# Inverse row sums of the attentions over 64 partitions by two DMAs through DRAM, not by products on PE

## What is computed

```
first block, each of 2 layers:
    q, k, v and gates of four branches from x @ w_in
    A: banded chunk attention with a relative bias, 4 heads    M: attention over 256 memory rows, 4 heads
    C: banded chunk attention with sinks, 4 heads              B: latent attention, chunk-causal, 4 heads
    y = concat(branch * silu(gate)) @ w_out;  x = layer_norm(alpha * x + y)
second block, each of 2 layers:
    Fourier mix of 512 channels, windowed attention with sinks over the other 512 (8 heads)
    x = x + concat(rms(y_f), rms(y_a)) @ w_o;  x = x + (silu(conv(gate)) * conv(val)) @ w_down
softmax of a head:  p = exp(s - max) / sum(exp(s - max));   out = p @ v
```

## Time and profile before

| | |
|---|---|
| median of the runs | 1791.63 us |
| time of the profiled execution | 1798.1 us |
| its span, first to last instruction | 1796.0 us |
| mean granted clock of TensorE | 0.963 of full |
| PE, DVE, ACT, POOL busy | 1721.2, 780.9, 695.8, 677.4 us |
| DMA | 145.90 MB, mean 81 GB/s |
| chain that ended last | PE 67%, issue 20%, POOL 7%, others 6% |

### The profile page before, as it was taken

The page is one execution under the profiler, slowest core; times in us unless marked ns, Lnnn a source line. Parts: engine busy times, 40 slices in busy tenths (PEclk is TensorE's granted clock), DMA queues, the critical chain, the costliest instruction groups (busy, mean ns, idle before and its releaser), DMA issues.

```text
span 1796.0 us, 24207 instructions
## 1 busy us (share of the span) xinstructions
PE 1721.2 (96%) x8858; PEld 1349.8 (75%) x8858; DVE 780.9 (43%) x1496; ACT 695.8 (39%) x1144; POOL 677.4 (38%) x523
## 2 busy tenths in 40 slices
PE   6999999999999979999999999999998999999999
PEld 5776567787656757877888888888776888888887
DVE  7225554501555363664455215432556355403541
ACT  4443462524446141554344223333345344313431
POOL 3431314443131352334444444434252544444443
PEclk9998998999999878998999999999998999999999
DMA  7220112222011112122232232223120322233222
GB/s 257 99 72 24 51 46 97 92 98 92 25 49 47 65 42 71 48 72 71 84 103 82 88 111 93 76 88 118 48 72 27 103 98 99 72 97 115 93 72 92
DMA packets 24608, 145.90 MB, mean 81 GB/s; under 512 B 3152, under 2 KB 3536, under 8 KB 10704
## 3 DMA queue, kind: packets, MB, share of 16 engines
q1 hardware_dynamic: 21840, 138.01, 22.4%
q10 hardware_dynamic: 2688, 6.82, 1.0%
HBM read 142.72 MB, written 2.10 MB: 81 GB/s over the span
## 4 chain that ended last, share of the span: by engine, by line
PE 67%; issue 20%; POOL 7%; ACT 2%; DVE 2%; DMA 1%; POOLq 0%; ACTq 0%; DVEq 0%
PE ring L513 58%; POOL w_lo L499 7%; PE scores L561 2%; PE ring L585 2%; PE outs L575 2%; PE ring L655 1%; PE ring L599 1%; DMA xt<-in_x 1%; PE ring L629 1%; PE ring L917 1%; ACT probs L1066 0%; ACT w_hi L1021 0%; ACT xh L1248 0%; ACT xt L1244 0%; DVE g L1561 0%
## 5 line engine op out<-in xcount | busy, mean ns | idle before, releaser
L499 POOL TENSOR_TENSOR w_lo<-w_stage,w_hi 128x258 fp32r<-128x258 f32 (+5 forms) x471 | 643.8, 1397 | 1075.5 <-ACT w_hi L1021 674.6
L513 PE MATMUL ring<-xh,w_lo 128*128 128x512 f32 x1296 | 521.3, 402 | 23.4 <-DVE w_lo L1439 10.7
L513 PE MATMUL ring<-xh,w_hi 128*128 128x512 f32 x1296 | 514.6, 397 | 0.0
L513 PE MATMUL ring<-xl,w_hi 128*128 128x512 f32 x1296 | 513.9, 397 | 0.0
L513 PEld LDWEIGHTS ring<-xh,w_lo 128*128 128x128 f32 x1296 | 246.4, 190 | 86.4 <-DVE w_lo L1439 10.7
L513 PEld LDWEIGHTS ring<-xh,w_hi 128*128 128x128 f32 x1296 | 246.2, 190 | 56.2
L513 PEld LDWEIGHTS ring<-xl,w_hi 128*128 128x128 f32 x1296 | 246.9, 191 | 53.5
L1370 ACT ACTIVATE w_hi<-w_stage 128x2048 fp32r<-128x2048 f32 (+2 forms) x70 | 116.6, 1666 | 158.8 <-PE ring L513 158.8
L1380 ACT ACTIVATE g<-ring,convw 128x512 f32<-128x512 f32 x88 | 68.1, 778 | 245.4 <-DVE ring L1871 245.4
L1021 ACT ACTIVATE w_hi<-w_stage 128x2064 fp32r<-128x2064 f32 (+2 forms) x81 | 123.5, 1537 | 95.0 <-PE ring L513 94.4
L1066 ACT ACTIVATE probs<-scores,neg_max 128x256 f32<-128x256 f32 (+2 forms) x192 | 96.1, 503 | 147.7 <-DVE neg_max L1533 36.4
(11 more groups left out here) (268 smaller groups left out, 2245.1 us busy)
## 6 DMA issues: line engine op xcount, KB each, us to landing
w_stage<-in_mixed SPq DMA_DIRECT2D x62, 1032.0 KB, 4.8
w_stage<-in_up SPq DMA_DIRECT2D x44, 1024.0 KB, 4.8
w_stage<-in_down SPq DMA_DIRECT2D x16, 768.0 KB, 4.2
w_stage<-in_down SPq DMA_DIRECT2D x16, 640.0 KB, 3.8
xt<-in_x ACTq DMA_DIRECT2D x4, 512.0 KB, 11.4
out_t<-xt ACTq DMA_DIRECT2D x8, 256.0 KB, 2.0
mem_f<-in_mem SPq DMA_DIRECT2D x1, 1024.0 KB, 9.6
bias_r<-in_relb SPq DMA_DIRECT2D x1, 1024.0 KB, 11.3
```

Of the source, the lines that this page charges most:

```text
L499: ins = nc.gpsimd.tensor_tensor(w_lo[:, slot, cols], source[:, cols], w_hi[:, slot, cols].bitcast(F32), ALU.subtract)
L513: ins = nc.tensor.matmul(o, lhs, rhs, start=start, stop=stop, skip_group_check=True)
```

## The change

Of each attention all output tiles but the last (o % 8 != 7 in the first block, o % 4 != 3 in the second; 20 of 24) get their rows in another way:

- ACT, one step after the last exponentials of the tile and behind the exponentials of that step, waits for the reciprocal and issues a DMA of the 128 x 8 inverse sums to a DRAM scratch of (2, 8, 128), transposed, so 1024 pieces of 4 bytes (`send_sums`).
- ACT, one step later and again behind the exponentials, waits until that DMA has landed and issues two DMAs that read 512 numbers of one head from the scratch onto 64 partitions each (`fetch_rows`). The rows go to `vb` or `raw`, which are free then, or in the second block straight to `g`.
- PE's `spread_heads` and its ring bank are gone for these tiles, in the second block ACT's copy of the bank too.
- DVE in the first block multiplies the output bank in place by the rows and then by the gate, two products one behind the other, in place of the product of gate and bank and the product of output and gate. All of it, and the work that follows it on ACT and DVE, is one step later than before; for tile 6 of a layer of the first block the split by ACT and DVE moves from the shared list of units to this place.

```diff
+def rows_by_dma(o):
+    return o % 8 != 7 if o < 8 * DEPTH else o % 4 != 3
@@ ring_plan and PE's attention
-            if t >= 2 and (t - 2) % TT == TT - 1:
+            if t >= 2 and (t - 2) % TT == TT - 1 and not rows_by_dma(pairs[t - 2][0]["o"]):
@@ build
+        sums_rows = nc.dram_tensor("sums_rows", (2, 8, P), F32).ap()
+        dma_tiles = [o for o in range(12 * DEPTH) if rows_by_dma(o)]
+        def row_buffer(o):
+            if o >= 8 * DEPTH:
+                return g[:, 4 + o % 4, :]
+            if o % 8 < 2:
+                return vb[:, 2 * (o % 2):2 * (o % 2) + 2, :].rearrange("p a b -> p (a b)")
+            return raw[:, 2 * (o % 2), :]
@@ ACT
+            def send_sums(o):
+                if rows_by_dma(o):
+                    act.wait_ge(S("inv_ready"), o + 1)
+                    act.dma_start(sums_rows[o % 2].rearrange("c q -> q c"), row_inv[:, o % 2, :],
+                                  allow_slow_non_contiguous=True).then_inc(S("sums_sent"), 16)
+            def fetch_rows(o, l):
+                if rows_by_dma(o):
+                    act.wait_ge(S("sums_sent"), 16 * (dma_tiles.index(o) + 1))
+                    if o < 8 * DEPTH and o % 8 == 2:
+                        act.wait_ge(S("lat_split"), 3 * l + 3)
+                    for par in range(2):
+                        act.dma_start(row_buffer(o)[64 * par:64 * par + 64, :], bass.AP(sums_rows.tensor, (o % 2 * 2 + par) * TOK, [[0, HD], [1, TOK]])
+                                      ).then_inc(S("rows_landed"), 16)
...
-                    if t >= 2 and (t - 2) % TT == TT - 1:
-                        take_sums(pairs[t - 2][0])
-                    if t >= 4 and (t - 4) % TT == TT - 1:
-                        after_out(pairs[t - 4][0])
+                    if 1 <= t <= N and pairs[t - 1][0]["qt"] == TT - 1:
+                        send_sums(pairs[t - 1][0]["o"])
+                    if 2 <= t <= N + 1 and pairs[t - 2][0]["qt"] == TT - 1:
+                        fetch_rows(pairs[t - 2][0]["o"], l)
+                        if not rows_by_dma(pairs[t - 2][0]["o"]):
+                            take_sums(pairs[t - 2][0])
+                    for late in (4, 5):
+                        if late <= t < N + late and (t - late) % TT == TT - 1 and rows_by_dma(pairs[t - late][0]["o"]) == (late == 5):
+                            after_out(pairs[t - late][0])
...
+                    act.wait_ge(S("out_taken"), 8 * l + 2)
                     for n in range(2):
                         for t in (2 * n, 2 * n + 1):
                             evac(("uv", l, t), vb[:, t, :], cols=slice(0, 256))
...
-                    for n in range(7):
+                    for n in range(6):
                         split_out(l, n)
@@ DVE
-                    if scale_gate and t >= 2 and (t - 2) % TT == TT - 1:
+                    if scale_gate and t >= 2 and (t - 2) % TT == TT - 1 and not rows_by_dma(pairs[t - 2][1]["o"]):
                         scale_gate(pairs[t - 2][1])
-                    if t >= 3 and (t - 3) % TT == TT - 1:
-                        finish(pairs[t - 3][1], 0)
-                    if t >= 4 and (t - 4) % TT == TT - 1:
-                        finish(pairs[t - 4][1], 1)
+                    for part in range(2):
+                        for late in (3 + part, 4 + part):
+                            if late <= t < N + late and (t - late) % TT == TT - 1 and rows_by_dma(pairs[t - late][1]["o"]) == (late == 4 + part):
+                                finish(pairs[t - late][1], part)
...
+            def rows_ready(it):
+                if rows_by_dma(it["o"]):
+                    dve.wait_ge(S("rows_landed"), 32 * (dma_tiles.index(it["o"]) + 1))
+                else:
+                    wait_taken(dve, ("bc", it["o"]))
+                dve.wait_ge(S("pv_done"), it["n"] + 1)
...
                     if part == 0:
-                        wait_taken(dve, ("bc", it["o"]))
-                        dve.wait_ge(S("pv_done"), it["n"] + 1)
+                        rows_ready(it)
+                        if rows_by_dma(it["o"]):
+                            gates_taken(n)
+                            o = o_bank[it["o"] % 2]
+                            step(v.tensor_tensor(o[:, :], o[:, :], row_buffer(it["o"]), ALU.mult))
                         v.tensor_tensor(g[:, tile, :], o_bank[it["o"] % 2][:, :], g[:, tile, :], ALU.mult).then_inc(S("out_taken"), 1)
```

More of the change, by code:

```diff
@@ L565, in attention @@
                         it = pair[0]
-                        if (t - 2) % TT == TT - 1:
+                        if (t - 2) % TT == TT - 1 and not rows_by_dma(it["o"]):
                             spread_heads(it["o"])
@@ L1052, in rotary_tables @@
                 act.wait_ge(S("sines"), 4)
+            def send_sums(o):
[11 more added lines that the diff above has]
+                                      ).then_inc(S("rows_landed"), 16)
             def attention(pairs, l, block, take_sums, after_out, between):
                 N = len(pairs)
-                for t in range(N + 4):
+                for t in range(N + 5):
                     if t >= 1:
@@ L1212, in later_projections @@
                             yield
-                attention(PAIRS[l], l, 1, lambda it: None, lambda it: split_out(l, 7) if it["o"] % 8 == 7 else None, later_projections())
+                attention(PAIRS[l], l, 1, lambda it: None, lambda it: split_out(l, it["o"] % 8) if it["o"] % 8 >= 6 else None, later_projections())
                 ahead = l + 1 < DEPTH
@@ L1638, in later_projections, with gates_taken @@
                             yield
-                def scale_gate(it):
-                    n, tile, name = it["o"] % 8, it["tile"], ("bc", it["o"])
+                def gates_taken(n):
                     if n in (0, 2):
@@ L1649, in scale_gate @@
                         wait_taken(dve, ("w", l, f"bg{n - 6}"))
+                def scale_gate(it):
+                    tile, name = it["tile"], ("bc", it["o"])
+                    gates_taken(it["o"] % 8)
                     wait_full(dve, name)
@@ L1655, in gate_pair @@
                     if part == 0:
-                        wait_taken(dve, ("bc", it["o"]))
-                        dve.wait_ge(S("pv_done"), it["n"] + 1)
+                        rows_ready(it)
[3 more added lines that the diff above has]
+                            step(v.tensor_tensor(o[:, :], o[:, :], row_buffer(it["o"]), ALU.mult))
                         v.tensor_tensor(g[:, tile, :], o_bank[it["o"] % 2][:, :], g[:, tile, :], ALU.mult).then_inc(S("out_taken"), 1)
-                    elif n == 7:
+                    elif n >= 6:
                         out_lo(l, n)
```

## The result

| | median of the runs | lowest to highest | runs |
|---|---|---|---|
| before | 1792.17 us | 1790.54 to 1794.35 | 4 |
| after | 1882.95 us | 1878.12 to 1887.09 | 4 |

After stands to before as 1.0509, with an interval of 1.0496 to 1.0522: 5.1% slower, where 0.7% faster was forecast. The profiled execution of the changed kernel has a span of 1882.2 us, against 1796.0 before.

The account below looks back on a forecast made before the run. Attentions were taken as bound mostly by PE's stream, in a few steps by ACT or DVE. Gross gain 24.4 us less 9.8, 1.2 and 0.4 gave 13 us: 1791.6 - 13 = 1778.6 us, range 1766 to 1792.

Parts of the forecast that it names:

- Part 5: Landing of the sums' 1024 pieces of 4 bytes in DRAM, which ACT awaits: 4 us taken, costing 0.4 us in all.
- high end: Upper estimate of the sums' landing: 64 pieces on each of 16 engines 6.8 us, with 2.0 us fixed 8.8 us.
- The rival: Landing late, ACT stands in the fetch and PE waits: 38 us lost on 12 tiles, 1817 us; chance 0.12.
- Part 1: PE's spreads in the attentions go: 20 at 0.93 us each, 18.6 us gained.
- The clock: PE's stretches at half clock could shift with the change: some +-4 us on the forecast time.
- Parts 2 to 4: Attentions: bank waits gone 5.8 us, ACT's added issues lose 9.8 us, DVE's moved products lose 1.2 us.
- C's first tile: First block: a fetch of 0.85 us with 0.5 us free pushes PE's scores from 238.20 to 238.7; 1.4 us lost.
- Part 4: DVE's two products stand together one step later: 0.6 us lost a layer, 1.2 in all; no wait for fetched rows.
- Part 2: PE's bank waits at the spreads go: 1.0 us and 1.9 us, each once a layer, 5.8 us gained.
- all of it is won: ACT's queue work overlaps its arithmetic and losses are half as large: gain 19 us, 1769 us; chance 0.10.
- The price of the send: ACT's issue of the sums' DMA: 0.35 to 0.45 us of its queue, up to 1 us with 1024 pieces.
- ACT becomes the bound: Queue instructions cost more, a send 1 us or more: 12 us go on 12 tiles, 1790 us, likelier 1785; chance 0.20.

## Why the prediction was wrong

**Part 5, the landing, is the step that failed.** The estimate of 4 us rested on two rows for large pieces. "I take 4 us, nearer to the store, since a 4-byte piece moves nearly nothing" chose the wrong side; measured were 8.5 to 12.3 us, 10.7 at the median. Even the high end of 8.8 us, from the queue's mean packet, was too low, and by a method that can't see it. The queue's packets in the changed kernel take 2.4% of 1882.2 us, 45.2 us, and with the pieces apart 2.5% of 1758.7, 44.0 us: the same, with landings of 10.7 and 2.6 us at the median. The time of the packets doesn't hold the delay; only the wait does. The sentence on the Trainium skill (DMA: Bandwidth & Descriptors, Specifications), that writes below 512 bytes are read, modified and written, was the one to price. It doesn't settle it either: all pieces at every distance are below 512 bytes, and they land in 1.4 to 12.4 us. The same page's 10.5 ns a packet (Bandwidth; there of loads), by which I had an estimate of 2.7 us, agrees with the pieces 64 or 512 bytes apart (2.8 and 2.6 us) and misses the change's own store by a factor of three to four and a half.

**The rival was the right mechanism, too small.** Its marks all came: DMA of the sums in the chain, ACT in the fetch, PE behind it. It gave 1817 us, for 12 tiles at 3.2 us. Measured is idle time of ACT on 18 tiles at 111.0 / 18 = 6.2 us (the fetch's issues in it), since at 10.7 us the long steps of A and of M's first tile don't cover the landing either; and I had counted nothing for the clock: for the same products PE's busy time has 505.1 - 461.7 = 43.4 us more than with the pieces apart. With the idle time, 106.8 - 27.8 = 79.0, this makes the 122.4 us between the two kernels' attentions. Its chance of 0.12 was too low: the one row against it, 2.0 us, was of a store in rows of 2 KB, and no row was of a store in pieces of 4 bytes.

**Parts 1 to 4**, held against the kernel with its pieces apart. Its span is 37.3 us shorter than before's (1796.0 - 1758.7), of which 32.5 are in the attentions: 29.2 us of PE's busy time and 3.3 of its idle time. Between medians it is 28.9: before's profiled execution lay 6.5 us above its median and at a clock of 0.963, where its other runs have 0.965 to 0.972. So up to some 7 us of what follows may be that one execution, and not the change.

- Part 1, 18.6 us for the spreads: held, as far as it can be told; the records of four tiles are left (64 of the 384). But 29.2 - 18.6 = 10.6 us more of PE's busy time went.
- The clock went with it. I had put it at +-4 us; the windows' granted clock rose from 0.92, 0.94, 0.97 and 0.96 to 0.98, 0.96, 1.00 and 0.99. No run here takes the clock by itself, so why it rose, and how much of the 10.6 us is the change's, is not shown. Outside the attentions another 4.8 us went (1274.0 - 1269.2), whose cause I haven't followed.
- Parts 2 to 4 together said +5.2 us of idle time (9.8 + 1.2 - 5.8); measured is -3.3. Two terms were too large. PE's waits for ACT's exponentials in the four windows rose from 7.8 to 13.0 us, and 1.4 us of waits for its `kb` turn up at another line, so ACT's losses are 6.6 us, not 9.8 (in C's first tile the recorded sum also slips: 238.20 + 0.35 is 238.55, not 238.7). And where Part 4 has DVE lose 1.2 us, PE's waits for the rotation's `tmp` before the units fell from 4.0 to 0.6 us; why isn't followed. Part 2's bank waits are gone as forecast. Why ACT loses less shows in the timeline of ACT in this kernel, C's first tile (start, us, engine, line; in brackets the idle time before):

```profile
221.46 0.47 ACT L1099 ACTIVATE probs<-scores,neg_max 128x256 f32<-128x256 f32 x1
221.46 0.47 ACTq L1084 DMA_DIRECT2D raw<-in_relb  x1
...
221.97 0.61 ACTq L1084 DMA_DIRECT2D raw<-in_relb  x1
222.28 0.20 ACT L1099 ACTIVATION_READ_ACCUMULATOR probs<-scores,neg_max 128x1 f32 x1
222.68 2.02 ACT L1037 ACTIVATE w_hi<-w_stage 128x1032 fp32r<-128x1032 f32 x2 [0.21 <-issue]
```

The issues run beside the exponentials that are already under way; the weight chunk starts 0.2 us late and not 0.85. That was the rival "all of it is won", in which ACT's queue work overlaps its arithmetic: its 1769 us is the nearest to what the change does once the landing is short (1762), though it too has nothing of the clock. Only where ACT has just waited does the fetch stand in its way in full, 243.13 to 244.34 in the changed kernel.
- The price of the send, 0.35 to 0.45 us, held: 0.37 at the median, 1024 pieces or not. The rival "ACT becomes the bound" needed 1 us or more there, and falls.
- DVE never waited for the fetched rows, as part 4 said.

## What to carry to other kernels

Keep writes of 4 bytes to DRAM from lying side by side: 64 bytes apart was enough here, and so was turning the tile first, so that each piece is 128 bytes; pieces of 32 bytes landed in 1.4 us. The time to landing of a small, strided store isn't in the profile's packet times nor in its KB; if a wait stands behind it, give it a range that reaches past 12 us, and look where the distance to the wait is shorter. A wait on an engine ahead of PE can cost twice, once as idle time and once in the clock behind it: here 79.0 and 43.4 us. Whether work taken off PE gives back more than its own time in the same way is not shown.

## What was not expected of the hardware

- 1024 pieces of 4 bytes land in 2.6 us (512 bytes apart), 2.8 (64), 5.0 (8), and 8.5 to 12.4 us side by side; 128 pieces of 32 bytes in 1.4 us. 256 pieces side by side still take 9.9 us.
- Such a store slows others. With the wait taken away and the pieces side by side, the weight queue's packets hold 24.6% of 1759.4 us, 433 us, against 22.6% of 1758.7, 397 us, with the pieces apart; and queue 10, with the fetches, 67 against 44 us. The other kernels fall in the same two groups: 435 us (23.1% of 1882.2) in the changed kernel, 450 (25.2% of 1783.9) with the fetch a step later and 434 (23.5% of 1848.1) with 32 bytes from one partition, all three side by side; 400 to 403 before the change, at 8 and 64 bytes and with the turn by DVE. That may be why the kernel without the wait has a median of 1769 and not 1762, but the two ratios' intervals overlap, so it isn't shown.
- The issue of a DMA by ACT hardly depends on the number of its pieces (0.37 us at 1024 of 4 bytes, 0.33 at 128 of 32; 0.57 for the three-dimensional pattern behind the turn), and runs beside ACT's arithmetic.
